# Second attention: GpSimd scales two neighbouring probability tiles in one multiplication with broadcast row factors

## The reference

```python
ss = jnp.einsum('bgrqd,bgqnkd->bgrqnk', qb, k_sel).astype(f32) - slopes[..., None] * d_s
ss = jnp.where(d_s >= 0, ss, NEG)
p_s = jax.nn.softmax(ss.reshape(ss.shape[:4] + (-1,)), axis=-1).reshape(ss.shape)
o_s = jnp.einsum('bgrqnk,bgqnkd->bgrqd', p_s, v_sel)
...
sw = jnp.einsum('bgrqd,bgkd->bgrqk', qb, kwb).astype(f32) - slopes * d_w
sw = jnp.where(ok, sw, NEG)
o_w = jnp.einsum('bgrqk,bgkd->bgrqd', jax.nn.softmax(sw, axis=-1), vwb)
gb = lax.dynamic_slice_in_dim(gates, q0, Q_BLOCK_2, axis=4)[..., None]
return gb[0] * o_c + gb[1] * o_s + gb[2] * o_w
```

## Time and profile before

| what | value |
|---|---|
| median of 3 runs | 3051.47 us (3051.4 to 3053.8) |
| profiled execution, its own time | 3050.31 us |
| its span in the profile | 3048.6 us |
| PE busy | 2992.0 us (98%) |
| DVE busy | 1699.2 us (56%) |
| ACT busy | 1109.4 us (36%) |
| POOL busy | 314.9 us (10%) |
| attention of the second block | about 2535 to 2630 us of the span |

### The profile page before, as it was taken

One profiled execution on the slowest core, in us unless ns is written; L12 is line 12 of the kernel. 1 busy time (PEld: TensorE's weight loads), 2 busy tenths in 40 slices (PEclk: granted clock), 3 DMA queues, 4 the chain that ended last, 5 costly groups with the idle time before them and its releaser, 6 DMA issues. The chain is left out here.

```text
span 3048.6 us, 37429 instructions
## 1 busy us (share of the span) xinstructions
PE 2992.0 (98%) x13534; PEld 2431.7 (80%) x13534; DVE 1699.2 (56%) x2387; ACT 1109.4 (36%) x1724; POOL 314.9 (10%) x254
## 2 busy tenths in 40 slices
PE   7999999999999999999999999999999999989999
PEld 6888888778888887888888888888888775678887
DVE  6555565565655556555556455555546767463334
ACT  4222333562332234322232455232223545552223
POOL 1000200000200024000030000200003215500000
PEclk9999999999999999999999999999999998999999
DMA  5242222113423222432233212333222420122322
GB/s 185 89 151 96 90 90 90 58 58 111 145 97 138 97 86 87 152 138 98 92 98 99 82 40 78 111 140 143 97 95 79 167 69 29 42 70 97 97 97 82
DMA packets 86809, 301.58 MB, mean 99 GB/s; under 512 B 10272, under 2 KB 19616, under 8 KB 85536
## 3 DMA queue, kind: packets, MB, share of 16 engines
q1 hardware_dynamic: 86688, 300.02, 29.4%
HBM read 297.88 MB, written 2.10 MB: 98 GB/s over the span
## 5 line engine op out<-in xcount | busy, mean ns | idle before, releaser
L1134 PE MATMUL proj<-u_hi,w_hi 128*128 128x512 f32 x2616 | 1027.9, 393 | 27.4 <-DVE u_lo L1590 19.7
L1136 PE MATMUL proj<-u_hi,w_lo 128*128 128x512 f32 x2616 | 1019.8, 390 | 0.0
L1135 PE MATMUL proj<-u_lo,w_hi 128*128 128x512 f32 x2616 | 1019.7, 390 | 0.0
L1585 DVE TENSOR_TENSOR w_lo<-raw,w_hi 128x1024 fp32r<-128x1024 f32 (+4 forms) x567 | 656.9, 1162 | 491.7 <-ACT w_hi L657 482.2
L657 ACT ACTIVATE w_hi<-raw 128x1024 fp32r<-128x1024 f32 (+4 forms) x567 | 536.3, 954 | 339.9 <-PE proj L1136 218.2
L1134 PEld LDWEIGHTS proj<-u_hi,w_hi 128*128 128x128 f32 x2616 | 492.1, 188 | 139.8 <-issue 22.9
L1135 PEld LDWEIGHTS proj<-u_lo,w_hi 128*128 128x128 f32 x2616 | 492.4, 188 | 103.7 <-issue 2.9
L1136 PEld LDWEIGHTS proj<-u_hi,w_lo 128*128 128x128 f32 x2616 | 492.2, 188 | 103.1
L1134 PE MATMUL proj<-a_hi,w_hi 128*128 128x512 f32 x936 | 368.1, 393 | 3.1 <-DVE w_lo L1585 1.5
L1136 PE MATMUL proj<-a_hi,w_lo 128*128 128x512 f32 x936 | 364.8, 390 | 0.0
L1135 PE MATMUL proj<-a_lo,w_hi 128*128 128x512 f32 x936 | 364.5, 389 | 0.0
(11 more groups left out here) (459 smaller groups left out, 2906.2 us busy)
## 6 DMA issues: line engine op xcount, KB each, us to landing
raw<-in_ffn_gu SPq DMA_DIRECT2D x174, 512.0 KB, 3.3
raw<-in_in_w SPq DMA_DIRECT2D x68, 512.0 KB, 3.3
raw<-in_ffn_dn SPq DMA_DIRECT2D x64, 512.0 KB, 3.3
raw<-in_ff SPq DMA_DIRECT2D x64, 512.0 KB, 3.4
gate<-in_ada SPq DMA_DIRECT2D x8, 3072.0 KB, 11.6
raw<-in_ffn_dn SPq DMA_DIRECT2D x32, 384.0 KB, 3.1
raw<-in_in SPq DMA_DIRECT2D x18, 512.0 KB, 3.4
raw<-in_mla_out SPq DMA_DIRECT2D x16, 512.0 KB, 3.4
```

The source lines that it names most:

```text
L1134: pe.matmul(out, w_h, x_h, start=first, stop=False)
L1135: pe.matmul(out, w_h, x_l, start=False, stop=False)
L1136: return pe.matmul(out, w_l, x_h, start=False, stop=last)
L1585: dve.tensor_tensor(wt(w_lo, slot, slot.tiles), wt(raw, slot, slot.tiles), wt(w_hi, slot, slot.tiles).bitcast(F32), ALU.subtract).then_inc ...
```

## The change

The loop in `scale` goes over i = 0 and 2. For each it multiplies a view of two tiles, [128, 2, width], by the two row factors that lie side by side in `row_stats`, broadcast along the width; the multiplication is a `tensor_tensor` with two inputs, where it was a `tensor_scalar` with one input and a scalar per row. It counts `p2_ready` up by 2 at once. The places of a pair must be neighbours: this is so for all but i = 0, 1 of every fourth step (`work` 0 and `ax` 13), which stay two single operations. The rest of the program is the same; its line numbers behind this place are 9 higher.

```diff
+        pair_at = lambda t, i: t[:, i * S:(i + 2) * S].rearrange("p (t s) -> p t s", t=2)
+        prob_pair = lambda g, i: (pair_at(work_t, 2 + 4 * (g % 4) + i) if g % 4 < 2 or g % 4 == 2 and i == 0 else
+                                  pair_at(ux_t, 14) if g % 4 == 2 else pair_at(ax_t, 8))[:, :, 0:(QT - g % QT) * P]
...
-                for i in range(4):
-                    pool.tensor_scalar(prob(g, i), prob(g, i), esum(g, i), None, ALU.mult).then_inc(p2_ready, 1)
+                for i in (0, 2):
+                    if g % 4 == 3 and i == 0:
+                        pool.tensor_scalar(prob(g, 0), prob(g, 0), esum(g, 0), None, ALU.mult).then_inc(p2_ready, 1)
+                        pool.tensor_scalar(prob(g, 1), prob(g, 1), esum(g, 1), None, ALU.mult).then_inc(p2_ready, 1)
+                        continue
+                    pair = prob_pair(g, i)
+                    pool.tensor_tensor(pair, pair, esum(g, i, 2).unsqueeze(2).to_broadcast([P, 2, (QT - g % QT) * P]), ALU.mult)\
+                        .then_inc(p2_ready, 2)
```

## The result

| what | before | changed |
|---|---|---|
| median of the runs, taken side by side (13 each) | 3053.8 us | 3059.15 us |
| ratio, 95% interval | | 1.0019 [1.0011, 1.0026] |
| profiled execution, its own time | 3050.31 us | 3061.7 us |
| its span in the profile | 3048.6 us | 3059.9 us |

The changed kernel is slower by 5.8 us, 3.4 to 7.9 by the interval.

A forecast was written before the change was run, and what follows sets the result against it. TensorE, 98% busy, was taken as the bound, with VectorE bounding the opening. 4.8 us in the opening plus 1.4 in the loop made 6.2: span 3054.8, median 3057.7 us; range 3051.0 to 3063.5.

The forecast's parts named there:

- TensorE doesn't wait for scaled tiles in the loop: Attention loop: step 9's last tile is scaled 2.9 us before its transpose group, so faster scaling buys nothing.
- At the end: Very last tile of the loop: scaled 0.2 us before its load on TensorE, so at most 0.2 us to gain.
- What a two-input operation holds: VectorE instructions with two SBUF inputs wait for GpSimd's whole two-input instruction, up to 2.35 us; one-input scalings hardly block.
- The price of a pair: GpSimd's two-tile multiplication: 2.35 us for 1024 columns and 1.80 for 2x384.
- (a): Opening: L1585 on VectorE is held by the first pair, delaying L2072 and what follows; 0.4 us (0 to 0.7).
- (b): Opening: the four L2197 alternate with GpSimd's pairs and L636; waits of 6.02 us, less 0.57 of today's.
- (c): Opening: GpSimd is done with L636 by the time of L2163, whose wait of 1.06 us goes.
- Loop: Second step of each head: L2018 waits 1.6 us in the first full head, 1.4 lost; 0.02 in the second, third likewise.
- the edge that I had called a knife's: Next two heads: rival where L2018 waits for the second pair, 2.2 us lost in each; 3062 us, 25%.
- No change: Rival: GpSimd's longer instruction is hidden, by an unread broadcast stream or one-input scalings holding VectorE equally; 3051.5 us, 17%.
- Faster: Rival: TensorE does wait for scaled tiles, so the pairs' saving counts in the loop, 3 to 4 us; 3048 us, 4%.
- A slow broadcast: Rival: broadcast costs half more a column, so holds are longer in opening and loop, 12 us; 3063.5 us, 9%.

The follow-up runs named there:

- the four profiles with these waits: Pairs at steps 0 and 1 only (1.0014); kernel before with u_lo moved (0.9992); single tiles with factors on GpSimd, with u_lo moved (1.0007) and without (1.0012).
- adding 1.2 us a head to GpSimd's work: Kernel before with the row factors multiplied on GpSimd instead of VectorE, single tiles throughout: 3058.0 us, 1.0012.
- The single two-input tiles: Against the kernel before: still one tile per scaling and signal, but as two-input multiplications with a broadcast factor; 3053.2 us, 1.0001.
- the loop-only run: Changed kernel with pairs from step 2 on only, single one-input scalings at steps 0 and 1; 3058.44 us, 1.0018 of the kernel before.
- the opening alone: Changed kernel with pairs at steps 0 and 1 only, one scaling per tile from step 2 on; 3056.87 us, 1.0014 of the kernel before.
- the low halves out of the way: Changed kernel with VectorE's four u_lo instructions (L2197, later L2206) moved from the opening to steps 7 and 11; 3055.5 us, 1.0000 of the kernel before.
- the two runs that take away the long pairs or the held instruction: Pairs from step 2 on: without those of 2 x 512 columns, 3052.3 us, 0.9995; with row factors multiplied on GpSimd, 3051.35 us, 0.9988 of the kernel before.
- with these cleared: Pairs from step 2 on, row factors multiplied on GpSimd, four u_lo instructions moved out of the opening; 3048.62 us, 0.9984 of the kernel before.
- moving the low halves alone: Kernel before with only VectorE's four u_lo instructions moved from the opening to steps 7 and 11; 3052.25 us, 0.9992.

## Why the prediction was right, and where it was not

The forecast of 3057.7 us was 1.5 below the 3059.15 measured. The runs of the kernel before that stand beside these had a median of 3053.8, not 3051.47, so the differences say more: 6.2 us forecast, 5.4 measured (5.8 by the ratio of the runs), 3.4 to 7.9 by the interval. The sum is right partly by luck, because terms failed in opposite directions: 2.0 us too much in the opening and 1.2 in the first full head, 2.1 too little in the two heads after it.

**TensorE doesn't wait for scaled tiles in the loop: right. At the end: wrong.** I had at most 0.2 us to be gained at the last tile, read from the earlier trace rows. The step that failed is that I took this margin from a profile in which TensorE's clock had fallen in the last head (0.57): TensorE was late there, and GpSimd had caught up. Where the clock stays up, GpSimd bounds the last head with single scalings, 14.32 us against 12.82 with a faster GpSimd, so 1.5 us are to be had up to the fourth start, and 1.7 to 3.0 more behind it, where the clock then falls. A fall of the clock early in the last head costs about the same as the waits (14.50 us at 0.88 in the changed kernel), and the two don't add, so it hides them. From the third start to the end of the span the four profiles with these waits take 441.9 to 445.1 us and all the others 438.4 to 439.2, the kernel before among them, with its early fall and hardly any of the waits. The profiled pair therefore doesn't show the gain; how much of it the medians hold is not shown. The 2.9 us of margin inside the loop was a thin one as well: adding 1.2 us a head to GpSimd's work was enough to make it the bound.

**What a two-input operation holds: right.** VectorE's instructions with two SBUF inputs wait for GpSimd's whole instruction and take turns with it. The single two-input tiles show that the kind of instruction does it, and the 2.55, 1.92 and 1.48 us in the changed kernel show that its length sets the price. The row that spoke against the Trainium skill (SBUF — State Buffer, "Who interferes with whom"), where any GpSimd instruction that reads SBUF contends with a two-input one of VectorE, holds up for one-input scalings too: with them the low halves take 0.74 to 1.07 us in the loop-only run.

**The price of a pair: too high.** 1.89 us in place of 2.35, and 1.47 in place of 1.80. It is below the lower bound that I had drawn from an addition of two full tiles (1292 ns for 512 columns; a broadcast of 512 takes 1038). A broadcast factor costs less here than a second full tile, and I had bounded it from one side only. GpSimd's busy time fell by 25.6 us where I said 15, from this term. It also set the next two points.

**Opening: 4.8 forecast, 2.8 measured** (2.77 with the opening alone, 3.0 in the changed kernel). (a) L1585 was forecast at 0.4 and is next to nothing: even where TensorE's clock is up, its delay fills VectorE's idle time ahead of L2072 and hardly more. In the run with the opening alone L1598 starts at 2541.53 and L2085 at 2544.01, 2.48 us later, against 2.43 in the earlier trace rows: 0.05 lost. (b) The low halves lost 7.4 - 3.5 = 3.9 in place of 5.45; the waits were those of shorter pairs. (c) L2163's 1.06 came back as forecast. 3.9 - 1.06 = 2.8 went into TensorE's time one to one, as I had counted it. The test of (b): with the low halves out of the way, the changed kernel's opening is 0.16 us from that of the other, and the kernel is at 1.0000 of the one before.

**Loop: 1.4 in the first full head and 0.02 in the next two forecast.** In the first one the wait is 0.53 us (L2027 takes 0.70 where it has 0.17 alone) and TensorE stands 0.17. In the next two, the edge that I had called a knife's falls the other way: 1.89 is less than 2.33, so L2018 came under the second pair, 1.31 us each, of which 1.06 reached the values. That rival had 2.2 us in each head, from a pair of 2.3; with pairs of 1.89 it is half of it. So in the loop the mechanism and the place were right, the case was the 25% one, and its price was off by the same term as above. That nothing else in the loop is at work was shown by the two runs that take away the long pairs or the held instruction: 17.93 and 17.72 us a head.

**Clock.** I had 1.7 us either way. The profiled execution had more: the stretch at 0.50 before the change begins (2.5 us lost), and 6.5 us at 0.50 behind the wait at 2598. Whether that wait brings the lower clock is open: with the loop alone the same wait of 0.99 stands before each of the three starts; behind the first the clock stayed at 1.00, behind the second it was down in part (0.72 and 0.80 in the 7 us after it), and the changed kernel with the low halves moved has a longer third head again, 22.27. But the kernel before shows a fall in its last head without any such wait.

**The rivals.** "No change" falls: both its reasons are refuted by the held rows. "Faster" came in an unforeseen form, as the gain at the end, too small to outweigh the holds; with these cleared the kernel is 5 us faster than before, of which moving the low halves alone may have given some 2.4 (0.9992, with no gain still in the interval). "A slow broadcast" was wrong in sign.

## What to carry to other kernels

Before making GpSimd's instructions fewer and longer, list VectorE's instructions with two SBUF inputs that can fall beside them, tiny ones too, and what is queued behind each: 0.17 us of work can wait for a whole instruction of the other engine. Then clear them away (move them to GpSimd itself, or to where VectorE has time) and only then fuse; here pairs went from 1.0019 to 0.9984 of the kernel before. And a margin read from one profile is only as good as the clock in that stretch: see the granted clock before saying that an engine has time to spare, and look behind the stage as well: the same waits cost as much again there.

## What the runs showed of the hardware

- A two-input multiplication on GpSimd whose second input is a factor broadcast along the columns takes 1.67 ns a column and 0.18 us, less than an addition of two full tiles (1292 ns for 512 columns) and less than the one-input scaling by a factor per row (1570 ns for 512).
- A one-input scaling on GpSimd (0.92 to 1.57 us) delayed VectorE's two-input instructions by 0.24 to 0.43 us (0.98, 1.07 and 1.18 against 0.74; 0.56 against 0.17), not by its own length.
- TensorE's granted clock falls to its lower level in different places in executions of programs that are the same up to there, with TensorE busy all the time: 0.50 from 2539 to 2542 in one profile, 1.00 in another.
- Where TensorE's last transposes each waited for a tile (four profiles), the granted clock fell in the last microseconds of these waits or just behind them, and the next fifty multiplications took 1.7 to 3.0 us longer than 7.85; in the ten profiles without these waits it was 1.00 there.
